# Spreading per-feature output scales over partitions: ones-times-diagonal matmuls, or a small store and a repeating load

## The reference

```python
def rms_norm_2(x, g):
    xf = x.astype(jnp.float32)
    y = xf * lax.rsqrt(jnp.mean(xf * xf, axis=-1, keepdims=True) + EPS)
    return (y * g.astype(jnp.float32)).astype(x.dtype)

for l in range(DEPTH_2):                      # two later layers
    mod = (silu(c) @ ada_w[l] + ada_b[l])     # 6 vectors of 1024: sh1, sc1, g1, sh2, sc2, g2
    modc = ...                                # the same six from c_ctx, for the context rows
    ...                                       # projections, attention, gmlp and conv branches
    y = mixer_merge(...)                      # 256 x 1024
    x = x + g1 * rms_norm_2(y, mix_post_g[l])
    h2 = modulate(rms_norm_2(x, ffn_pre_g[l]), sh2, sc2)
    x = x + g2 * rms_norm_2(sq_relu_mlp(h2, w_ff1[l], w_ff2[l]), ffn_post_g[l])
    if not last:
        ...                                   # the same for the context rows xc, with gc1 and gc2
```

## Time and profile before

| | |
|---|---|
| median of three runs | 2932.4 us |
| profiled execution | 2928.34 us |
| span in its trace | 2926.5 us |
| TensorE busy | 2817.5 us (96%) |
| VectorE busy | 1468.9 us (50%) |
| ScalarE busy | 490.5 us (17%) |
| GpSimd busy | 84.3 us (3%) |
| mean granted TensorE clock | 0.987 |

### The profile page before, as it was taken

The page is one execution under the profiler, slowest core; times in us unless marked ns, Lnnn a source line. Parts: engine busy times, 40 slices in busy tenths (PEclk is TensorE's granted clock), DMA queues, the critical chain, the costliest instruction groups (busy, mean ns, idle before and its releaser), DMA issues.

```text
span 2926.5 us, 34786 instructions
## 1 busy us (share of the span) xinstructions
PE 2817.5 (96%) x13298; PEld 1907.7 (65%) x13298; DVE 1468.9 (50%) x3187; ACT 490.5 (17%) x989; POOL 84.3 (3%) x111
## 2 busy tenths in 40 slices
PE   4989999999999999999999999999999999999998
PEld 2555455555555545544587578688888867587897
DVE  6764111444452031111378854476664778755666
ACT  1222101122211010000112131110110120311211
POOL 0000000000000000000100000000000000011000
PEclk9989999999999999999999999999999999999999
DMA  8557999999999989999853413423331643145442
GB/s 343 220 242 289 378 420 412 409 407 405 404 402 403 404 366 420 416 412 418 326 206 142 168 66 138 143 115 116 115 115 64 246 151 144 58 158 189 156 173 87
DMA packets 108789, 749.73 MB, mean 256 GB/s; under 512 B 12785, under 2 KB 13169, under 8 KB 21585
## 3 DMA queue, kind: packets, MB, share of 16 engines
q1 hardware_dynamic: 92736, 682.66, 58.6%
q0 software_dynamic: 8816, 50.07, 4.6%
q10 hardware_dynamic: 7072, 14.76, 1.3%
HBM read 737.22 MB, written 10.22 MB: 255 GB/s over the span
## 4 chain that ended last, share of the span: by engine, by line
PE 89%; DVE 7%; DMA 2%; ACT 1%; issue 1%; SPq 0%; DVEq 0%; ACTq 0%
PE ps L696 18%; PE ps L1021 14%; PE ps L1430 9%; PE ps L1436 9%; PE ps L930 8%; PE ps L1184 8%; PE ps L708 7%; PE ps L926 3%; PE ps L1394 2%; PE ps L1382 1%; PE ps L728 1%; PE ps L757 1%; DMA ring<-stream 1%; PE ps L1031 1%; PE ps L1076 1%
## 5 line engine op out<-in xcount | busy, mean ns | idle before, releaser
L696 PE MATMUL ps<-area,ring 128*128 128x256 f32 x2432 | 533.5, 382 | 0.3
L696 PEld LDWEIGHTS ps<-area,ring 128*128 128x128 f32 x2432 | 465.2, 192 | 65.9 <-DVE area L2404 1.1
L1021 PE MATMUL ps<-ring,area 128*64 128x512 f32 x1784 | 395.9, 596 | 2.7 <-DMA ring<-stream 2.6
L1021 PEld LDWEIGHTS ps<-ring,area 128*64 128x64 f32 x1784 | 125.5, 137 | 267.8 <-issue 259.1
L930 PE MATMUL ps<-area,ring 128*128 128x256 f32 x1024 | 226.4, 379 | 0.0
L930 PEld LDWEIGHTS ps<-area,ring 128*128 128x128 f32 x1024 | 192.1, 190 | 24.9
L2347 DVE SCALAR_TENSOR_TENSOR area<-area,cols 128x256 f32<-128x256 f32 x480 | 201.9, 486 | 1.1
L1184 PE MATMUL ps<-ring,area 128*64 128x512 f32 x872 | 196.6, 600 | 4.3 <-ACT area L2982 4.3
L708 PE MATMUL ps<-ring,area 128*128 128x512 f32 x448 | 194.1, 593 | 0.0
L1430 PE MATMUL ps<-ring,area 128*128 128x256 f32 x768 | 173.1, 379 | 0.0
L1430 PEld LDWEIGHTS ps<-ring,area 128*128 128x128 f32 x768 | 145.6, 190 | 19.7
(11 more groups left out here) (413 smaller groups left out, 2942.7 us busy)
## 6 DMA issues: line engine op xcount, KB each, us to landing
ring<-stream SPq DMA_DIRECT2D x584, 1024.0 KB, 9.2
area<-stream SPq DMA_DIRECT2D x42, 1024.0 KB, 10.7
area<-shared_modulation POOLq DMA_DIRECT2D x32, 1024.0 KB, 5.5
area<-modulation SPq DMA_DIRECT2D x16, 1536.0 KB, 6.7
expert_rows<-area ACTq DMA_DIRECT2D x62, 128.0 KB, 7.2
area<-stream POOLq DMA_DIRECT2D x4, 1024.0 KB, 15.3
x<-x_tiles ACTq DMA_DIRECT2D x1, 1024.0 KB, 12.8
area<-ctx_tiles ACTq DMA_DIRECT2D x1, 1024.0 KB, 4.9
```

Of the source, the lines that this page charges most:

```text
L696: i = mm(ps[:, b, 0:n], w[:, k % 4, j * P:(j + 1) * P], rhs(k), start=(k == 0), stop=(k == 4 * kgs - 1))
L1021: i = mm(ps[half(h), bank, :], xT[:, k % 4, half(k // 4)], w[:, 2 * (k % 2) + h, :], start=False, stop=(k == KD - 1))
```

## The change

The diagonals, the ones-times-diagonal matmuls and ScalarE's copies go. GpSimd stores each `aff` column as a row of 1024 values in a DRAM tensor (`store_gains`), and later loads that row 128 times over into `bcv` (`spread_gains`), behind a wait until the stores have landed. `residual` waits for that load in place of the copies.

```diff
+        gains_d = nc.dram_tensor("gain_rows", (LAYERS, 2, 2, D), F32).ap()
...
+        gains_stored = K.sem("gain_rows_stored")
+        gains_spread = K.sem("gain_rows_spread")
+        SPREAD = {(0, 0): 1, (0, 1): 3, (1, 0): 4, (1, 1): 5}
...
@@ TensorE
-                def spread(which):
-
-                    for s in range(nf // 2 if which else 1):
-                        for g in range(2):
-                            b = claim("all" if which else "aux", (L, "bc", which, s, g))
-                            for j in range(4):
-                                k = 4 * g + j
-                                pe.wait_ge(*at((L, "dg", which, s, k)))
-                                i = mm(ps[:, b, j * P:(j + 1) * P], ones, dgb[which][:, KD * s + k], start=True, stop=True)
-                            i.then_inc(*mark("spread_full", ("full", (L, "bc", which, s, g))))
...
-                branch("conv", cv, [(L, "cvn", k) for k in range(KD)], lambda: spread(0))
+                branch("conv", cv, [(L, "cvn", k) for k in range(KD)])
...
-                    if i == 4:
-                        spread(1)
@@ VectorE
-                def diagonals(which):
-                    for s in range(nf // 2 if which else 1):
-                        for k in range(KD):
-                            TS(dgb[which][:, KD * s + k], ident, aff[:, 4 + 2 * which + s, k:k + 1], None, ALU.mult).then_inc(*mark("diagonals", (L, "dg", which, s, k)))
-                diagonals(0)
...
-                    for g in range(2):
-                        dve.wait_ge(*at(("drained", (L, "bc", which, t // 2, g))))
+                    dve.wait_ge(gains_spread, 16 * SPREAD[l, which])
...
-                diagonals(1)
@@ ScalarE
-                            A(bcv[:, s, 512 * g:512 * g + 512], ps[:, B((L, "bc", which, s, g)), :], ACT.Identity).then_inc(*mark("spread_copied", ("drained", (L, "bc", which, s, g))))
...
@@ GpSimd
+                def store_gains(which):
+
+                    for s in range(TT if which and l == 0 else 1):
+                        pool.wait_ge(*at(("gain", l, which, s)))
+                        with nc.allow_non_contiguous_dma(reason="one column of gains to a row"):
+                            pool.dma_start(gains_d[l, which, s].rearrange("(k p) -> p k", p=P), aff[:, 4 + 2 * which + s]).then_inc(gains_stored, 16)
+
+                def spread_gains(which):
+
+                    pool.wait_ge(gains_stored, 16 * SPREAD[l, which])
+                    for s in range(TT if which and l == 0 else 1):
+                        pool.dma_start(bcv[:, s, :], gains_d[l, which, s:s + 1].to_broadcast([P, D])).then_inc(gains_spread, 16)
+                if l == 0:
+                    store_gains(0)
                 for br in ("attn", "conv"):
                     for f in range(KD):
+                        if (br, f) == ("attn", 0) and l:
+                            store_gains(0)
+                        if (br, f) == ("conv", 1):
+                            pool.wait_ge(*at((L, "cvn", KD - 1)))
+                            spread_gains(0)
                         pool.wait_ge(*at(("drained", ((L, "out", br), f))))
...
+                store_gains(1)
+                for t in range(TT):
+                    pool.wait_ge(*at((L, "x1", t)))
+                spread_gains(1)
```

More of the change, by code:

```diff
@@ L2285, in coefficients @@
                             if f0 <= gate_ < f1:
-                                TT_(aff[:, at_ + s], modb[:, s, gate_:gate_ + 8], col((gain, l), 0, 8), ALU.mult).then_inc(*mark("vector_steps"))
+                                TT_(aff[:, at_ + s], modb[:, s, gate_:gate_ + 8], col((gain, l), 0, 8), ALU.mult).then_inc(*mark("vector_steps", ("gain", l, at_ // 2 - 2, s)))
                                 dve.wait_ge(*last("vector_steps"))
@@ L3124, in _ @@
                 gates("conv", range(4), lambda f: ("drained", ((L, "out", "attn"), f + 4)))
-                def spread(which):
-                    for s in range(nf // 2 if which else 1):
-                        for g in range(2):
-                            act.wait_ge(*at(("full", (L, "bc", which, s, g))))
-                            A(bcv[:, s, 512 * g:512 * g + 512], ps[:, B((L, "bc", which, s, g)), :], ACT.Identity).then_inc(*mark("spread_copied", ("drained", (L, "bc", which, s, g))))
-                spread(0)
                 gates("conv", range(4, KD), None)
@@ L3156, in _ @@
                 for n, i in enumerate(GROUPS):
-                    if i == 5:
-                        spread(1)
                     act.wait_ge(*at((L, "made", i, 1)))
```

## The result

The changed kernel takes 2914.97 us (2912.46 to 2917.81, 4 runs) against 2932.85 us of the kernel before on the same chip: ratio 0.9944, 95% interval 0.9930 to 0.9958. That is 16.4 us less (12.3 to 20.5); the two medians lie 17.9 us apart. The profiled execution took 2917.81 us, its span 2916.0 us, 10.5 us less than the span before.

What follows compares the result with a forecast made beforehand. TensorE, busy 96% of the span, was taken to bound the kernel. Savings of 8.92 (TensorE), 3.14 (VectorE) and 0.47 us (banks), nought elsewhere, sum to 12.53 us: 2932.4 less 12.5 gives 2919.9 us, range 2916 to 2927.

Steps and rivals of the forecast that it cites:

- the sum: The whole kernel: 8.92 us from TensorE, 3.14 from VectorE and 0.47 from banks, a saving of 12.53 us.
- TensorE's part: Both layers' conv branches, layer 0's unit 4, layer 1's units: 40 matmuls (80 instructions) go, saving 8.92 us in full.
- VectorE's part: Of 40 diagonals only the 16 ahead of layer 0's unit 1 count: 3.14 us saved, 0.21 us of wait stays.
- Banks: Layer 1's unit 1: another bank removes a 0.47 us wait; from layer 0 to 1: nought, 0.5 us as bad end.
- GpSimd's part: Five stores and five repeating loads: covered, no cost; the store matters only in layer 0, ahead of chunk 24's load.
- E: Time one store keeps GpSimd, in layer 0: taken as 2 us, between 0.53 and 7.55 us.
- S: A store's way to DRAM, in layer 0: taken as 3 us, between 2.3 and 9.1 us.
- the formula: Layer 0's chunk 24 lands at 1916.05 + 2E + S, wanted by VectorE at 1920.41: a stand of 2.7 us.
- The spare 11.0 us: Layer 0, behind chunk 24's steps: a VectorE stand below 11 us costs nothing before unit 2's fourth product.
- the case: Layer 0's queue behind the stores: chunk 24 exceeds the cover; gain reduced (middle 2924 us, chance 0.12) or slower (0.06).
- the argument that up to 2.4 us of delay are hidden: Layer 1: the repeating load delays a chunk load, hidden by VectorE's 2.44 us wait for a later-issued load.
- the prediction's signs of being wrong: TensorE waiting in layer 0's unit 2, a 9 us store, a layer-change wait above 2.61 us, or a grown layer 1 wait.

Runs made afterwards that it cites:

- the products kept: The changed kernel with TensorE's 40 ones-times-ones products left in their five places, read by nobody, with their PSUM banks: 2923.30 us, 8.1 us over the changed kernel.
- The sixteen: The changed kernel with only the 16 diagonals ahead of layer 0's unit 1 kept on VectorE, stores issued behind them: 2921.66 us; with TensorE's wait filled, 2916.08 us.
- the two more places: The changed kernel with the context's output scale and last experts' gate scale also stored and loaded over DRAM, by ScalarE's queue: 2919.76 us, ratio 0.9966.
- after: The first profile of the changed kernel, no further edit; that timing's median is 2914.97 us, ratio 0.9944.

## Why the prediction was right, and where it was off

The mechanism held. The time, 2914.97 us, lies 4.9 us below the 2919.9 forecast and 1.0 us below the range; by the ratio (0.9944 of 2932.4 us, 2916.0) it stands on the range's edge. The range was narrow on this side: it allowed 3.9 us for a saving above the sum. The profiled execution was forecast at 2915.8 us and took 2917.81; 1.95 of these 2.0 us had been lost in the untouched expert part before the later layers began (1744.01 and 1742.06 us).

- *TensorE's part*, 8.92 us: right. The stages give 1.79 in layer 0's conv branch, 3.57 at unit 4 and 1.89 in layer 1's units; the fourth place lies in the middle stage, which varies. With the products kept everything came back in the table, 9.7 us with the bank's 0.65, and 8.1 us in the medians.
- *VectorE's part*, 3.14 us: **the mis-sized term.** The wait fell from 3.35 to 0.22 us, 3.13. But in its stage the wait was worth more than its length: in three of the four profiles that have it, another 1.7 to 2.9 us went to half clock in the products behind it, 1.6 us on average over the four. The sixteen cost 6.4 us by the medians, and 0.8 us with TensorE kept at work in the wait; the second is less than the 3.1 us that the trace shows, so neither may be read to the microsecond. I took the price from one profile, which happened to show the clock at 1.00. That the other groups of diagonals bring nothing is not cleanly shown: keeping all 40 cost 0.4 us more in the medians than keeping 16, and the middle stage varies by more.
- *Banks*: the 0.47 us went, and the gap is 0.65 us shorter with them. From layer 0 to layer 1 the shift came out at the nought expected: 5.32 us before and 5.31 after from the last product to the first projection, with the wait of 2.61 us now 1.73 us and ahead of the turns.
- *GpSimd's part*: right in its result in layer 0, with luck in it, since both unknowns were wrong in opposite directions. E was 0.92 us (taken 2), S 8.0 to 11.4 us, median 9.9 (taken 3, high end 9.1). S was too low because I argued that queues nearly empty would land a store sooner than the 7.2 us of the earlier trace rows. With the 12.0 us measured from the scales to the end of the store's wait for 2E + S, the formula gives a stand of 7.6 us; it was 6.68, as the load landed 7.6 us after its issue began and not 8.5. The spare 11.0 us, on which the case hung, was confirmed to 0.3 us. In layer 1 the argument that up to 2.4 us of delay are hidden was not enough: the wait at the modulation sums, one of the prediction's signs of being wrong, grew from 0.33 us to 0.50 to 1.93 in nine of twelve profiles. The sum has no term for it, and whether the change causes it is open.
- The Trainium skill (DMA: Bandwidth & Descriptors, Rules for kernel authors) has a strided last dimension at one descriptor per element; I had made 4.2 us of GpSimd's time of it. The measured 0.92 us decides against that estimate. The packets of GpSimd's queue (packets, MB, share), before and after:

```profile
q0 software_dynamic: 8816, 50.07, 4.6%
```
```profile
q0 software_dynamic: 9696, 52.72, 4.8%
```

  Of the 880 more, 640 are the five loads' 128 rows, if each is one packet, which leaves 48 for a store of 1024 values. With the two more places, the same kind of store goes through ScalarE's queue, here in *after* and in that kernel:

```profile
q10 hardware_dynamic: 7072, 14.76, 1.3%
```
```profile
q10 hardware_dynamic: 9440, 15.82, 1.5%
```

  These are 2368 more. Less 256 for the rows of two loads, that is 1056 for each store, about one for each value. So one value, one packet holds on that queue and not on GpSimd's; what its 48 packets hold no run shows. What is slow on both is the landing.
- *From the profile to the median*: no stage shows missed work for the surplus over the sum. Two profiles of each kernel differ by 12.4 to 16.5 us in the later layers, and the medians by 14.7 and 17.9 us in the two timings. The two profiles of the kernel before are 3.5 us apart, with 6.8 us more at half clock in the slower. In the changed kernel's two, *half* is 17.1 and 10.2 us and yet they are 0.5 us apart, with the wait of 1.60 us on the other side. How much of the surplus falls to unit 1's wait and how much to other stretches stays open.

## What to carry to other kernels

Price a wait of a saturated TensorE by its length and by the clock of the work behind it, and look at more than one profile: here 3.35 us cost up to 6.3 in their stage. A round trip over DRAM for 4 KB is paid in landing time (about 10 us on GpSimd's queue beside half-idle DMA engines, 27 to 31 on ScalarE's beside a full weight stream), so it is free only where tens of microseconds of cover stand; count the cover of what is queued behind it, too. Here work taken off the bounding engine counted in full, and work off another engine only where the first waited for it.

## What was unexpected

- A filled wait keeps the granted clock at 1.00, but the stretches of half clock saved in one place turned up behind other waits, and neither the total at half clock nor the time moved.
- Unit 1's diagonals and GpSimd's DMA issue side by side slowed one 268 ns operation to 744 ns.
- A 4 KB store of separate values landed later (9.9 us at the median) than a 1 MB load of the same kernel on the same queue (5.9 us). In layer 0's units, where two of the five stores lie, the DMA engines are busy to a third.
